# A decoder trunk step with 32 experts on one Trainium2 core: one fixed expert round moved behind the loop, its rows added by a one-hot product

## The reference

```python
g_idx = argmax(g_logits)                       # 1 of 4 groups
top_v, top_i = lax.top_k(e_sel, 2)             # 2 of 8 experts in it
top_w = softmax(top_v) * p_g
for g in range(4):
    h1 = einsum('td,edf->tef', xt, exp_w1[g]); h3 = einsum('td,edf->tef', xt, exp_w3[g])
    act = silu(h1) * h3 * comb[:, g, :, None]
    out = out + einsum('tef,efd->td', act, exp_w2[g])
y = rms_norm(x + out, final_norm_g)
```

## Time and profile before

| what | value |
|---|---|
| median of three runs | 661.59 us |
| the profiled execution, its own time | 662.47 us |
| its span, first to last instruction | 660.7 us |
| busy in the span: PE, DVE, ACT, POOL | 598.9, 324.8, 186.4, 71.2 us |
| DMA traffic | 179.46 MB, mean 272 GB/s |
| expert rounds on PE | 410.7 to 635.1 us |
| from the last product of the rounds to the end | 25.6 us |

### The profile page before, as it was taken

How to read it: one execution, slowest core, us unless ns; L and a number is a source line. 1 busy time by engine, 2 the same in 40 slices (tenths; PEclk the granted TensorE clock), 3 DMA queues, 4 the chain that set the end, 5 groups by cost and what they waited for, 6 DMA issues and landing times.

```text
span 660.7 us, 11996 instructions
## 1 busy us (share of the span) xinstructions
PE 598.9 (91%) x4918; PEld 476.6 (72%) x4918; DVE 324.8 (49%) x668; ACT 186.4 (28%) x319; POOL 71.2 (11%) x144
## 2 busy tenths in 40 slices
PE   8999999999999999998999989998999999578930
PEld 8999997677899999984788878555655556236610
DVE  5669799889643464676713165312212221112116
ACT  5523223245834344436003050111011101000103
POOL 1000000000002200000302211211121111102010
PEclk9999999999999999999999998999999999979985
DMA  8762210326554223659769688899999999999927
GB/s 321 295 282 92 101 65 2 131 87 215 167 159 170 101 92 129 255 217 377 299 239 395 260 310 330 353 416 417 418 421 419 420 420 419 420 420 420 400 97 314
DMA packets 35523, 179.46 MB, mean 272 GB/s; under 512 B 8967, under 2 KB 10407, under 8 KB 16645
## 3 DMA queue, kind: packets, MB, share of 16 engines
q1 hardware_dynamic: 26317, 163.19, 62.7%
q0 software_dynamic: 5600, 12.76, 5.0%
q10 hardware_dynamic: 3552, 2.75, 1.3%
HBM read 172.85 MB, written 15.61 MB: 285 GB/s over the span
## 4 chain that ended last, share of the span: by engine, by line
PE 72%; DMA 11%; DVE 6%; issue 5%; SPq 4%; ACT 1%; POOL 0%; DVEq 0%; POOLq 0%; ACTq 0%
PE ps L2228 13%; PE ps L1779 13%; PE ps L1781 12%; PE ps L1780 12%; PE ps L2257 7%; DMA w<-exp_w 4%; PE ps L1893 4%; PE ps L1775 3%; SPq L660 3%; DMA q_rows<-q_s 2%; DMA raw<-weights 2%; DMA qb<-q_rows 2%; PE ps L1850 1%; DMA yr<-y_rows 1%; PE ps L2059 1%
## 5 line engine op out<-in xcount | busy, mean ns | idle before, releaser
L1779 PE MATMUL ps<-xH,w_h 128*128 128x260 f32 x480 | 138.3, 288 | 0.3 <-DVE xL L1417 0.3
L1781 PE MATMUL ps<-xL,w_h 128*128 128x260 f32 x480 | 135.6, 283 | 0.0
L1780 PE MATMUL ps<-xH,w_l 128*128 128x260 f32 x480 | 135.4, 282 | 0.0
L2228 PE MATMUL ps<-w,xeT 128*64 128x256 f32 (+2 forms) x1024 | 116.9, 390 | 9.5 <-DMA w<-exp_w 7.3
L2228 PEld LDWEIGHTS ps<-w,xeT 128*64 128x64 f32 (+2 forms) x1024 | 80.8, 139 | 49.1 <-issue 21.9
L1779 PEld LDWEIGHTS ps<-xH,w_h 128*128 128x128 f32 x480 | 90.4, 188 | 5.1 <-issue 4.3
L1780 PEld LDWEIGHTS ps<-xH,w_l 128*128 128x128 f32 x480 | 90.3, 188 | 0.3 <-issue 0.2
L1781 PEld LDWEIGHTS ps<-xL,w_h 128*128 128x128 f32 x480 | 90.4, 188 | 0.0
L1098 DVE TENSOR_TENSOR w_l<-raw,w_h 128x2048 fp32r<-128x2048 f32 x27 | 61.8, 2288 | 28.2 <-ACT w_h L779 28.1
L2257 PE MATMUL ps<-w,aT 128*64 128x512 f32 (+2 forms) x256 | 60.3, 627 | 15.8 <-DVE aT L1688 12.7
L779 ACT ACTIVATE w_h<-raw 128x2048 fp32r<-128x2048 f32 x27 | 51.6, 1911 | 21.9 <-PE ps L1781 18.9
(11 more groups left out here) (375 smaller groups left out, 862.3 us busy)
## 6 DMA issues: line engine op xcount, KB each, us to landing
w<-exp_w SPq DMA_DIRECT2D x96, 1024.0 KB, 22.6
raw<-weights SPq DMA_DIRECT2D x27, 1024.0 KB, 5.3
raw<-caches SPq DMA_DIRECT2D x16, 1024.0 KB, 6.1
qb<-q_rows POOLq DMA_DIRECT2D x4, 1024.0 KB, 7.5
yr<-y_rows SPq DMA_DIRECT2D x4, 1024.0 KB, 8.4
xT<-x_turned SPq DMA_DIRECT2D x4, 520.0 KB, 7.5
raw<-x_prompt SPq DMA_DIRECT2D x4, 512.0 KB, 12.4
x_rows<-x ACTq DMA_DIRECT2D x4, 512.0 KB
```

Source lines behind the costliest of these rows:

```text
L1779: pe.matmul(out, h1, h2, start=start, stop=False)
L1780: pe.matmul(out, l1, h2, start=False, stop=False)
L1781: return pe.matmul(out, h1, l2, start=False, stop=stop)
L2228: last = pe.matmul((mm[0][half, j, 0:FF], ta[1][half, 0:FF])[h], xeT[j][:, k, half], w13[s][:, h, k, :], start=k == 0, stop=k == KT_D - 1)
```

## The change

The fixed rounds become "PPPPPQSSQSQSP": 13 instead of 14, with three Q rounds in place of two, so 15 rounds in all. The last of them (places 26 and 27), called the late round, is not run with the fixed ones: twelve fixed rounds, then the loop's pass of two, then the late round.

- The late round's weights are the last that SP loads, behind the loop's (slots 2 and 3, `FREE_AT[2]` = 11 finished rounds). The loop's own loads use slots 5, 6, 0 and 1 and wait for 10 and 11 finished rounds.
- Its row buffer is `xe[2]`. POOL first scatters that buffer, filled with zeros, to the late round's places in `y_rows`, ahead of all gathers into it. It gathers the late rows in the body of q = 11, after a wait for the scatters of that buffer (the zeros and rounds 2, 6 and 10). PE turns them into a third column tile ahead of the loop.
- Its finished rows are not scattered. DVE makes a one-hot matrix from the token numbers; PE multiplies it with the rows (8 products of 128x512 for the prompt, 9 small ones for the samples) into PSUM.
- SP reads `y_rows` back as soon as the loop's scatters have landed. POOL, behind its waits for the loop's gathers, adds the two rows of each token (4 adds of 128x1024); DVE adds the late product to that sum. The loads of the final gain move behind the second tile's read. The sample tokens' part of the end moves behind the third tile.

```diff
-for kind in "PPPPSPPPSQSPQS":
+for kind in "PPPPPQSSQSQSP":
...
+LATE = PAIRS - 1
+LATE_PLACES = ROUNDS[LATE]
+LOOP_J = (LATE % 2, (LATE + 1) % 2)
...
-FREE_AT = [max(ROUND_OF[FIXED + 2 * r + n - RING] for n in range(2)) + 1 for r in range(2)]
+BEFORE_LOOP = LATE_PLACES[0]
+LOOP_SLOTS = [(BEFORE_LOOP + n) % RING for n in range(4)]
+LATE_SLOTS = [(BEFORE_LOOP + 4 + n) % RING for n in range(2)]
+FREE_AT = [max(ROUND_OF[BEFORE_LOOP + 2 * r + n - RING] for n in range(2)) + 1 for r in range(3)]
...
+        LATE_ROWS = (LATE + 2) % ROWS
...
         def scattered(i, q):
+            return len(range(i, q, ROWS)) + int(i == LATE_ROWS)
+        def gathered(i, q):
             return len(range(i, q, ROWS))
...
+            which = [expert_at(p) for p in LATE_PLACES]
+            for h, free in enumerate((gate_ready, hid_ready)):
+                sp.wait_ge(free, FREE_AT[2])
+                for i, e in zip(LATE_SLOTS, which):
+                    load_half(i, e, h)
+            sp.wait_ge(y_done, FREE_AT[2])
+            for i, e in zip(LATE_SLOTS, which):
+                load_down(i, e)
...
             for t, (t0, n) in enumerate(TILES[:4]):
                 sp.dma_start(yr[t][:], rows[t0:t0 + n]).then_inc(yr_in[t], 16)
+                if t == 1:
+                    sp.dma_start(fin_g[:], a["final_norm_g"].rearrange("(o d) -> o d", o=1).broadcast_to([P, D])).then_inc(fg_in, 16)
+                    sp.dma_start(fin_gs[0:N_PARTS], a["final_g_parts"]).then_inc(fg_in, 16)
...
+            dve.wait_ge(route_made, 6)
+            link(dve.tensor_copy(late_no[:], gids[:, LATE:LATE + 1]))
+            dve.tensor_scalar(hot_late[:], token_row[:, 0:SEQ], late_no[:, 0:1], None, ALU.is_equal)
...
+            late = loops_n * 2 + LATE
+            gate_of(late, LOOP_J[0], of_slot[:, 0, LATE:LATE + 1])
+            act_columns_out(late)
+            rows_out(late, LATE_ROWS, of_slot[:, 1, LATE:LATE + 1])
+            def add_late(t):
+                dve.wait_ge(y_pair, t + 1)
+                dve.wait_ge(y_total, t + 1)
+                row = x2[:, t, :].rearrange("p (b f) -> p b f", b=2)
+                dve.tensor_tensor(row, late_sums(t)[:], row, ALU.add).then_inc(y_sum, 1)
...
+            add_late(0)
             dve.wait_ge(fg_in, 32)
+            for t in range(3):
+                add_late(t + 1)
+                dve.wait_ge(y_sq, t + 1)
+                mean_of(fin_ss[:, t:t + 1], fin_ss[:, t:t + 1])
+                factor_of(fin_ss[:, t:t + 1], t + 1)
+                normed(t, slice(0, D))
...
-            for q in range(PAIRS):
+            for q in range(LATE):
                 hidden(q, q % 2, slots_of(q), q >= 2, slot_lists if q == 0 else None)
...
+            gathered_columns(LATE_ROWS, gathered(LATE_ROWS, LATE) + 1)
             pe.wait_ge(pass_ready, 1)
             loops_n = pe.value_load(more[0:1, 0:1], min_val=1, max_val=MORE_ITEMS // 4)
+            pe.wait_ge(xa_ready, LATE + 1)
+            pe.wait_ge(xv_ready, LATE + 1)
             with pe.Fori(0, loops_n) as it:
...
+            hidden(late, LOOP_J[0], slots, turned=(LATE + 1, xeT[2]))
+            act_columns(late)
+            down(late, slots)
+            def late_rows(t, b):
+                return pe.matmul(late_sums(t)[:, b, :], hot_late[:, t * P:(t + 1) * P], xe[LATE_ROWS][:, 512 * b:512 * b + 512],
+                                 start=True, stop=True)
...
             pool.wait_ge(xe_zero, ROWS)
-            for q in range(PAIRS):
+            scatter(LATE_ROWS, ids[:, LATE:LATE + 1])
+            for q in range(LATE):
                 pool.wait_ge(xt_done, q + 1)
-                i = (q + 2) % ROWS
-                if q + 2 >= ROWS:
+                i, column = (q + 2) % ROWS, q + 2 + int(q + 2 >= LATE)
+                if scattered(i, q + 2):
                     pool.wait_ge(y_stored[i], 16 * scattered(i, q + 2))
-                gather(i, gids[:, q + 2:q + 3])
+                gather(i, gids[:, column:column + 1])
+                if q == LATE - 1:
+                    pool.wait_ge(y_stored[LATE_ROWS], 16 * scattered(LATE_ROWS, LATE))
+                    gather(LATE_ROWS, gids[:, LATE:LATE + 1])
                 pool.wait_ge(y_ready, 2 * (q + 1))
                 scatter(q % ROWS, ids[:, q:q + 1])
+            pool.memset(hot_s_rows[:, 0:NS * NS * NS], 0.0).then_inc(route_made, 1)
+            pool.iota(token_row[:], pattern=[[1, T]], base=0, channel_multiplier=0,
...
             for i in LOOP_ROWS:
-                wait(xe_landed[i], loops_n * 16 + 16 * (scattered(i, PAIRS) + 1))
+                wait(xe_landed[i], loops_n * 16 + 16 * (gathered(i, LATE) + 1))
+            for t in range(4):
+                pool.wait_ge(yr_in[t], 16)
+                pool.tensor_tensor(x2[:, t, :], yr[t][:, 0, :], yr[t][:, 1, :], ALU.add).then_inc(y_pair, 1)
```

More of the change, by code:

```diff
@@ L701, in _ @@
             sp.wait_ge(order_ready, 1)
[L702 to L703 removed]
+            for q, places in enumerate(ROUNDS[:LATE]):
+                coming = [p + RING for p in places if p + RING < BEFORE_LOOP]
                 if coming:
@@ L1914, in conv_taps @@
                 for g in range(2):
-                    for k in range(TAPS - LATE, TAPS):
+                    for k in range(TAPS - LAST_TAPS, TAPS):
                         for r in (2 * g, 2 * g + 1):
@@ L2213, in gathered_columns, with hidden @@
                 last.then_inc(xt_done, 1)
-            def hidden(q, j, loads, old=True, between=None):
-                pe.wait_ge(xa_ready, q + 1)
-                pe.wait_ge(xv_ready, q + 1)
+            def hidden(q, j, loads, old=True, between=None, turned=None):
+                n_turned, columns = turned or (q + 1, xeT[j])
+                pe.wait_ge(xa_ready, n_turned)
+                pe.wait_ge(xv_ready, n_turned)
                 if old:
@@ L2290, in _ @@
-            pe.wait_ge(y_sq, 1)
+                slots = [(i, it + ((BEFORE_LOOP + n) // RING + 1)) for n, i in enumerate(LOOP_SLOTS)]
+                gathered_columns(LOOP_ROWS[0], it + (LATE // ROWS + 1))
+                hidden(it * 2 + LATE, LOOP_J[0], slots[0:2], turned=(it * 2 + (LATE + 2), xeT[LOOP_J[0]]))
+                gathered_columns(LOOP_ROWS[1], it + ((LATE + 1) // ROWS + 1))
+                act_columns(it * 2 + LATE)
+                down(it * 2 + LATE, slots[0:2])
+                hidden(it * 2 + (LATE + 1), LOOP_J[1], slots[2:4], turned=(it * 2 + (LATE + 3), xeT[LOOP_J[1]]))
@@ new lines, in _ @@
+                act_columns(it * 2 + (LATE + 1))
+                down(it * 2 + (LATE + 1), slots[2:4])
+            late = loops_n * 2 + LATE
+            slots = [(i, (BEFORE_LOOP + 4 + n) // RING + 1) for n, i in enumerate(LATE_SLOTS)]
+            hidden(late, LOOP_J[0], slots, turned=(LATE + 1, xeT[2]))
[4 more added lines that the diff above has]
+                                 start=True, stop=True)
@@ new lines, in _ @@
+            pe.wait_ge(y_ready, loops_n * 4 + (2 * LATE + 1))
+            late_rows(0, 0)
+            late_rows(1, 0)
+            pe.wait_ge(y_ready, loops_n * 4 + (2 * LATE + 2))
+            late_rows(0, 1).then_inc(y_total, 1)
+            late_rows(1, 1).then_inc(y_total, 1)
+            for t in (2, 3):
+                if t == 3:
+                    pe.wait_ge(y_sum, 1)
+                for b in range(2):
+                    last = late_rows(t, b)
+                last.then_inc(y_total, 1)
@@ L2291, in _ @@
+            pe.wait_ge(yr_in[4], 16)
+            pe.matmul(ta[1][0:N_PARTS, 0:PART], two_rows[:].rearrange("p t c -> p (t c)"), yr_s[:], start=True, stop=False)
+            for c in range(NS):
+                last = pe.matmul(ta[1][0:N_PARTS, 0:PART], hot_s_rows[:, c * NS * NS:(c + 1) * NS * NS], xe[LATE_ROWS][:, c * PART:(c + 1) * PART], start=False,
+                                 stop=c == NS - 1)
+            last.then_inc(y_total, 1)
+            pe.wait_ge(y_sq, 4)
             pe.matmul(ta[0][0:N_PARTS, 0:1], same_token[:].rearrange("p t c -> p (t c)"), fin_ss[0:N_PARTS, 4:5], start=True,
```

195 lines of the change are left out of this document (99 added, 96 removed).

## The result

The changed kernel takes 672.68 us in the median of four runs (670.16 to 675.21), the kernel before 661.9 us in four: a ratio of 1.0156, with a 95% interval of 1.0126 to 1.0187. It is slower by 10.8 us; 13 were forecast. The profiled execution of the changed kernel took 670.16 us, with a span of 668.4.

A forecast was written before the change was run, and what follows sets the result against it. PE and DMA were both taken as full, the weight stream until 627 us, PE pacing the end. Loop's end 640.5 (587 + 20.6 + 5.3 + 25.6 + 2.0), plus tail 33.3 and 0.9, gives 675 us; range 660 to 680.

The forecast's parts named there:

- The weight stream: Expert rounds: weight loads decide when the last Q round, round 10, ends: 584.5 us, ten microseconds before its counterpart.
- Load 77: The w2 load of the last Q round, round 10; that round's last product was to start at its landing, 579.1.
- PE ahead of the stream: Rival: round 10 does not wait for its w2 and ends at PE's own pace, 557; time 652, chance 0.13.
- The early wait: Round 1: round 2's gather waits for the zeros' scatter; PE stands still 8.8 us, DMA idles 2.5 (bounds 0, 8.8).
- The late gather: Ahead of the loop: it waits for round 10's scatter, landing 20.6 us behind that round; PE stands still 8.3 us.
- gathers hidden: Rival: scatters and gathers land in a few us, so both new waits vanish; time 662, chance 0.18.
- The loop's entry: Ahead of the loop: two turnings with no round to hide them, 5.34 us; slow first products add 2.0.
- The rounds: All rounds to the loop's end: at 640.5, 5.4 us later than the whole of the rounds before.
- The tail: Loop's end to span's end: late round, reading back, POOL's sums and DVE's chain take 33.3 us, against 25.6 before.
- No second pass: Rival at the loop: experts overflow the twelve places and a second pass costs 30 us; chance under 1 in 100.

The follow-up runs named there:

- run 5: Changed kernel with the old mix of rounds (PPPPSPPPSQSQSP, two Q rounds, 16 rounds with the late one); ratio 1.0116 to the kernel before.
- run 1: Changed kernel with the late places' zeros scattered out of xe[3] instead of xe[2]; ratio 1.0081 to the kernel before.
- Run 2: Changed kernel with PE turning the late rows behind the loop instead of ahead of it; ratio 1.0003 to the kernel before.
- the swapped order: Changed kernel with one pair of rounds swapped (PPPPPQSSQSSQP); ratio 0.9994 to the kernel before; 0.9912 with run 4's three edits added.
- run 7: Changed kernel with useless products on PE during the late wait; ratio to the kernel before 1.0121 with 20 products, 1.0137 with 30.
- run 3: Changed kernel with POOL adding the row pairs before waiting for the loop's two unused gathers; ratio 1.0133 to the kernel before.
- run 4: Changed kernel with the edits of run 1, Run 2 and run 3 together; 658.34 us, ratio 0.9938 to the kernel before.

## Why the prediction was right

The forecast was 675 us, slower with 0.71; it came out at 672.7, slower. Step by step, times from the rounds' start (410.7 in the forecast):

- **The weight stream.** Load 77 was to land 170.9 us behind the rounds' start (579.1 + 2.5 - 410.7) and to let round 10 end at 176.3. It landed at 578.3, which is 170.7, and the round ended at 174.5. But PE did not wait for it: its last wait for weights ended at 571.0, for w3, and it was ready for the last product 0.2 us behind load 77's landing. So that product ran at full speed (3.64 us for the 5.34 of the sum). That the stream sets this end is shown by run 5: with another round of 12.7 us in front, it moves by 1.2 us. The rival "PE ahead of the stream" falls with it.
- **The early wait.** I said 8.8 us of standing still and 2.5 us lost. PE stood for 6.5 us, as the gather landed in 8.0 us instead of 10.6 (the scatter took 8.5, said 8.2), and then ran slowly for 3.1 us more, which I had left out. The next loads came at 446.0, and the hole was 3.7 us wide. Removing the wait took 4.9 us off round 10's end: the term was mis-sized by half, inside its bounds of 0 and 8.8.
- **Luck in the two together.** Without the early wait load 77 would have come at 168.4 by the sum; in run 1 PE's wait for it ended at 166.0. The stream was 2.4 us ahead of my count and the early wait held load 77 up by 4.7 us (166.0 to 170.7), 2.2 more than I took, so their sum was right where neither was.
- **The late gather.** Landing at 20.6 us behind round 10, said; 19.2 measured (582.1 to 601.3), a wait of 6.7 for 8.3. Run 2 and the swapped order both show that this wait, and not the number of rounds, kept the loop back. The rival "gathers hidden" falls: round 10's scatter and the late gather took 8.6 and 8.2 us from issue to landing, inside the full stream. The fit that the Trainium skill gives for such a DMA (DMA: Bandwidth & Descriptors, Anatomy of one DMA), 3.2 us by estimate, does not hold while another queue keeps the engines full. One of my reasons against that rival was a misreading: that a gather took 8.1 us "even with an idle queue". It was issued at 640.23, amid four reads of 1 MB that went out from 639.52. The changed kernel's first unused gather, issued at 638.53 ahead of such reads, landed in 2.3 us, its second, behind two of them, in 7.5. What counts against the rival are the landings inside the full stream.
- **The loop's entry and the clock.** Two bare turnings were there as said. The lowered clock cost 3.6 us (run 7), not 2.0.
- **The rounds.** The loop's end: 229.8 said, 228.0 measured. The errors (round 10's end 1.8 us earlier, the late rows 1.4 sooner behind it, and 1.4 more from their landing to the loop's end, for the clock) partly cancel.
- **The tail.** 33.3 us said, 32.8 measured. POOL's first sum came 13.6 us behind the loop's end (13.2 said), the four took 10.3 us (10.4 said), DVE waited for them. The Trainium skill's statement that GpSimd contends with VectorE's instructions of two SBUF inputs (GPSIMD Engine Reference, Specifications) agrees with the rows: the scaling, with two SBUF inputs, takes 1.55 and 1.63 us beside POOL's sums and 1.28 behind them, and one of the sums took 3.3 us instead of 2.35, while DVE's late adds, with one input from PSUM, take 1.22 us beside the sums too. Together it is about 1 us, far from the 10 that I had left room for. With the sums first it grows: the first scaling took 1.92 us in run 3, 3.21 in run 4 and 2.35 with the order swapped.
- **No second pass** of the loop ran.

What comes next in the tail once POOL's sums start earlier, run 3 shows: PE's late product, for which DVE waits 2.1 us. Open stays why the rounds start between 407.6 and 412.2 us in kernels that are equal up to there.

## What to carry to other kernels

When a stage is fed by a saturated stream, count what has to have landed for each step before counting rounds: here a whole round more or less on the engine was worth under 1 us in the stretches. A buffer taken over for a new purpose brings its last user's landing with it: look up who wrote it last, how long a landing takes **under that load**, and what covers it; a move to another buffer, a move of the consumer by one step and the sums ahead of an idle wait turned a loss of 1.6% into a gain of 0.6%, and 0.9% with two rounds swapped. And a wait for something that nobody uses (the last gathers of a loop) belongs behind the work, not ahead of it. Last, a ratio can agree with a theory that the timeline refutes (run 7): look for the mechanism in the trace before believing the time.

## What the runs showed of the hardware

- A stall's cost is not its length. After 6.7 us of idle time PE ran at 1.2 GHz for some 10 us more, across short bursts and gaps of 1.4 us, and gave away 3.6 us. Keeping it busy until the landing avoided that; stopping 2.35 us short did not. A row of short gaps can do the same without a stall: with gaps of 1.57, 1.42 and 1.52 us between two turnings of 1.16 us the clock fell from 2.4 to 1.2 GHz (order swapped, 589 to 596 us).
- In a stream at 420 GB/s an indirect gather or scatter of 0.5 MB took 7.6 to 11.5 us to land. A gather of nothing of use took 2.3 us with the DMA engines idle and 7.5 behind two reads of 1 MB (changed kernel), so what else is in flight decides, and not only what it moves.
- Side by side, GpSimd's adds and VectorE's scaling, which has two SBUF inputs, took longer, one or both of them: the scaling 1.55 to 3.21 us instead of 1.28, one add in each run 3.2 to 3.3 instead of 2.35.
- Four runs of the changed kernel lay 5 us apart (670.16 to 675.21), where the four of the kernel before lay 2.6 apart, and in the later batches 14 to 17 runs of the kernel before spread over 5 to 7 us, so effects of 2 or 3 us could only be settled in the traces.
